# Sums over w_ada for the second layer and both gates: products by ScalarE, additions by GpSimd

## What is computed

```python
mod = jax.nn.silu(c) @ w_ada + b_ada
shift, scale, gate = jnp.split(mod[:, None, :], 3, axis=-1)
h = rms_norm(x, norm_g) * (1 + scale) + shift
z = h @ w_in                       # eight parts: queries, keys, values, gates, latents
o_mla, o_moba = ...                # two attentions of 8 heads
y = jnp.concatenate([silu(g_mla) * o_mla, silu(g_moba) * o_moba], axis=-1) @ w_out
return x + gate * y
```

## Time and profile before

| | |
|---|---|
| median of 3 runs | 1597.88 us (1596.69 to 1599.29) |
| profiled execution | 1596.89 us |
| its span, first to last instruction | 1594.7 us |
| TensorE busy | 1552.5 us (97%) |
| VectorE busy | 1069.9 us (67%) |
| ScalarE busy | 869.8 us (55%) |
| GpSimd busy | 117.0 us (7%) |
| chain that ended last | PE 88%, DVE 5%, ACT 3%, issue 2%, DMA 1% |
| loads of w_ada | 48 of 512 KB, median 5.3 us from issue to landing |

### The profile page before, as it was taken

How to read it: one execution, slowest core, us unless ns; L and a number is a source line. 1 busy time by engine, 2 the same in 40 slices (tenths; PEclk the granted TensorE clock), 3 DMA queues, 4 the chain that set the end, 5 groups by cost and what they waited for, 6 DMA issues and landing times.

```text
span 1594.7 us, 21371 instructions
## 1 busy us (share of the span) xinstructions
PE 1552.5 (97%) x7540; PEld 1290.8 (81%) x7540; DVE 1069.9 (67%) x1789; ACT 869.8 (55%) x1534; POOL 117.0 (7%) x142
## 2 busy tenths in 40 slices
PE   4989999999999999999999999999999999999998
PEld 4777887788888888888888888888888888888886
DVE  7987877666555766787756557565666578766553
ACT  3676667455445656565644446444566666554442
POOL 0310021011000000021000001000000002100000
PEclk9999999999999999999999999999999999999999
DMA  9964673379854634546565557975463444665651
GB/s 340 322 233 158 196 239 128 104 180 221 222 185 158 198 96 133 174 141 213 197 200 170 198 184 197 199 205 192 158 199 118 139 160 147 211 207 172 205 184 71
DMA packets 149026, 293.03 MB, mean 184 GB/s; under 512 B 10096, under 2 KB 23184, under 8 KB 148920
## 3 DMA queue, kind: packets, MB, share of 16 engines
q1 hardware_dynamic: 143424, 276.60, 51.5%
q0 software_dynamic: 4352, 12.15, 6.2%
q10 hardware_dynamic: 1144, 2.92, 0.5%
HBM read 290.57 MB, written 1.06 MB: 183 GB/s over the span
## 4 chain that ended last, share of the span: by engine, by line
PE 88%; DVE 5%; ACT 3%; issue 2%; DMA 1%; POOL 0%; DVEq 0%; SPq 0%; ACTq 0%
PE pb L475 83%; PE pb L479 5%; DMA raw<-in_w_ada 1%; DVE wl L1529 1%; ACT wh L906 1%; ACT pb L906 1%; DVE mkv L1526 1%; POOL st L2461 0%; DMA raw<-in_w_in 0%; DVE qt L1526 0%; ACT xt_h L906 0%; DVE mk L1529 0%; ACT mkv L906 0%; DVE B L1529 0%; DVE pb L1532 0%
## 5 line engine op out<-in xcount | busy, mean ns | idle before, releaser
L906 ACT ACTIVATE wh<-raw 128x1024 fp32r<-128x1024 f32 (+1 forms) x484 | 506.5, 1053 | 424.6 <-PE pb L475 394.2
L1529 DVE TENSOR_TENSOR wl<-raw,wh 128x1024 fp32r<-128x1024 f32 (+1 forms) x484 | 581.4, 1218 | 197.6 <-ACT wh L906 193.6
L475 PE MATMUL pb<-wh,xt_h 128*128 128x512 f32 (+2 forms) x1472 | 578.1, 393 | 4.0 <-ACT xt_h L906 2.5
L475 PE MATMUL pb<-wh,xt_l 128*128 128x512 f32 (+2 forms) x1472 | 572.4, 389 | 1.4 <-DVE xt_l L1529 1.0
L475 PE MATMUL pb<-wl,xt_h 128*128 128x512 f32 (+2 forms) x1472 | 569.6, 387 | 0.0
L475 PEld LDWEIGHTS pb<-wh,xt_l 128*128 128x128 f32 x1472 | 277.1, 188 | 64.1 <-DVE xt_l L1526 5.9
L475 PEld LDWEIGHTS pb<-wh,xt_h 128*128 128x128 f32 x1472 | 277.2, 188 | 59.5 <-issue 4.0
L475 PEld LDWEIGHTS pb<-wl,xt_h 128*128 128x128 f32 x1472 | 277.4, 188 | 52.5
L475 PE MATMUL pb<-wh,big_h 128*128 128x512 f32 x352 | 137.7, 391 | 0.0
L475 PE MATMUL pb<-wh,big_l 128*128 128x512 f32 x352 | 137.0, 389 | 0.0
L475 PE MATMUL pb<-wl,big_h 128*128 128x512 f32 x352 | 137.0, 389 | 0.0
(11 more groups left out here) (242 smaller groups left out, 1546.5 us busy)
## 6 DMA issues: line engine op xcount, KB each, us to landing
raw<-in_ffn_w_gu SPq DMA_DIRECT2D x160, 512.0 KB, 4.9
raw<-in_w_in SPq DMA_DIRECT2D x148, 512.0 KB, 4.3
raw<-in_ffn_w_down SPq DMA_DIRECT2D x88, 512.0 KB, 3.9
raw<-in_w_ada SPq DMA_DIRECT2D x48, 512.0 KB, 5.3
raw<-in_w_out SPq DMA_DIRECT2D x32, 512.0 KB, 4.1
raw<-in_w_branch SPq DMA_DIRECT2D x24, 512.0 KB, 4.2
raw<-in_ffn_w_gu SPq DMA_DIRECT2D x32, 256.0 KB, 4.9
raw<-in_w_in SPq DMA_DIRECT2D x8, 416.0 KB, 4.8
```

The source lines that it names most:

```text
L475: return e.matmul(o, a, b, start=start, stop=stop)
L906: return e.activation(o, a, func, **kw)
L1529: return e.tensor_tensor(o, a, b, op)
```

## The change

The tiles (0, 0) and (0, 2) stay as they are. For the four others, 32 rows, the work moves from VectorE to two engines. ScalarE multiplies a row by its weights (`weigh` in act): for kx = 0 into the accumulator, for the others in place, raw into raw; the signal is ("prod", l, j, kx). It stands in ScalarE's queue where the row stands in the plan, right behind the copy of the entry before it. GpSimd adds raw to the accumulator for kx = 1 to 7 (`sums`), signal ("accp", l, j, kx); for kx = 0 it only waits for the product. A buffer is free for the next load after "prod" for kx = 0 and after "accp" for the others. Where the additions stand in GpSimd's order is written out by hand: SUMS gives for each layer how many rows are done after the rs of rn, before those of qb, before those of kb, before those of mq, and after the load of the gate's bias: 4, 2, 2, 9, 7 in the first layer and 3, 1, 2, 2, 0 in the second. What TensorE waits for before it adds up over the partitions is changed accordingly.

```diff
--- before.py
+++ after.py
@@ -399,12 +399,16 @@
 
     def weighed(l, j, kx):
 
-        return ("acc", l, j + 1 if j < 4 and l == 0 and kx == 7 else j, kx)
+        if (l, j) in ((0, 0), (0, 2)):
+            return ("acc", l, j + 1 if kx == 7 else j, kx)
+        return ("accp", l, j, kx) if kx else ("prod", l, j, 0)
 
     def first_bank_of(c):
 
         return {0: 2, 2: 3, 4: 7}.get(c)
 
+
+    SUMS = ((4, 2, 2, 9, 7), (3, 1, 2, 2, 0))
 
     def moba_unit(l):
         def f(hh, t):
@@ -666,7 +670,7 @@
             if j >= 4:
                 return
             b = rot("mod", l, j)
-            w.wait_ge(*at("acc", l, j // 2 * 2 if l else j, 7))
+            w.wait_ge(*(at("accp", l, j // 2 * 2, 7) if l else at("acc", l, j, 7)))
             w.wait_ge(*at("ones"))
             a = acc_of[l, j // 2 * 2][:, j % 2 * 512:j % 2 * 512 + 512]
             for f in range(4):
@@ -763,7 +767,7 @@
             later.drain(0 if l else 8)
             for j2 in range(2):
                 o = open_bank(first_bank + j2, ("gate", l, j2))
-                w.wait_ge(*at("acc", l, 4, 7))
+                w.wait_ge(*at("accp", l, 4, 7))
                 mm(o, ones[:, :], acc_of[l, 4][:, j2 * 512:j2 * 512 + 512], True, True).then_inc(*up("turn", l, 4 + j2))
             side.drain()
             later.over(7)
@@ -913,11 +917,23 @@
             for c in chunks:
                 src, kk, n, _, i, ada_ = plan[c]
                 if ada_:
+                    if ada_[0:2] not in ((0, 0), (0, 2)):
+                        weigh(c)
                     continue
                 w.wait_ge(*at(f"raw{c % NRAW}", c))
                 if i >= NW:
                     w.wait_ge(*at(*plan[split_at[i - NW]][3]))
                 ac_(wh[i % NW][:, 0:kk * n], raw[c % NRAW][:, 0:kk * n]).then_inc(*up("hi", c))
+
+        def weigh(c):
+
+            l, j, kx = plan[c][5]
+            v = raw[c % NRAW][:, :]
+            w.wait_ge(*at(f"raw{c % NRAW}", c))
+            w.wait_ge(*at("csil"))
+            if kx == 0 and (l, j) in acc_free:
+                w.wait_ge(*at(*acc_free[l, j]))
+            ac_(v if kx else acc_of[l, j], v, scale=stat(8, "c_silu")[:, kx:kx + 1]).then_inc(*up("prod", l, j, kx))
 
         def turn_of_temp(reader):
 
@@ -1540,7 +1556,8 @@
             for c in chunks:
                 src, kk, n, _, i, ada_ = plan[c]
                 if ada_:
-                    weigh(c)
+                    if ada_[0:2] in ((0, 0), (0, 2)):
+                        weigh(c)
                     continue
                 w.wait_ge(*at("hi", c))
                 if i >= NW:
@@ -1553,17 +1570,14 @@
 
 
             l, j, kx = plan[c][5]
-            first = l == 0 and j < 4
             v, a = raw[c % NRAW][:, :], acc_of[l, j]
             weight = stat(8, "c_silu")[:, kx:kx + 1]
             w.wait_ge(*at(f"raw{c % NRAW}", c))
             if kx == 0:
-                if (l, j) in acc_free:
-                    w.wait_ge(*at(*acc_free[l, j]))
                 ts(a, v, weight, None, ALU.mult, None).then_inc(*up("acc", l, j, 0))
                 return
             w.wait_ge(*at("acc", l, j, kx - 1))
-            if kx < 7 or not first:
+            if kx < 7:
                 stt(a, v, weight, a, ALU.mult, ALU.add).then_inc(*up("acc", l, j, kx))
                 return
             for z in range(2):
@@ -2477,6 +2491,19 @@
                 e.dma_start(bc[:, a0:a0 + n], bass.AP(tensor=d[name].tensor, offset=0, ap=[[0, 128], [1, n]])).then_inc(
                     *landed(to))
 
+        def sums(n):
+
+            for _ in range(n):
+                c, (l, j, kx) = rows_left.popleft()
+                w.wait_ge(*at("prod", l, j, kx))
+                if kx > 1:
+                    w.wait_ge(*at("accp", l, j, kx - 1))
+                if kx:
+                    a = acc_of[l, j]
+                    e.tensor_tensor(a, a, raw[c % NRAW][:, :], ALU.add).then_inc(*up("accp", l, j, kx))
+
+        rows_left = deque((c, p[5]) for c, p in enumerate(plan) if p[5] and p[5][0:2] not in ((0, 0), (0, 2)))
+
         e.memset(ones[:, :], 1.0).then_inc(*up("ones"))
         e.memset(cols[:, 126:128], -0.5).then_inc(*up("half"))
         e.memset(gp[:, :], 1.0).then_inc(*up("gpone"))
@@ -2487,6 +2514,7 @@
         for l in range(NL):
             for t in range(2):
                 rstd(1, "rn", l, t)
+            sums(SUMS[l][0])
             for t in range(2):
                 rstd(1, "zq", l, t)
                 rstd(1, "zk", l, t)
@@ -2497,10 +2525,12 @@
                 e.dma_start(gv, bass.AP(tensor=scratch.tensor, offset=0, ap=[[1, 128], [512, 8], [1, 256]])).then_inc(
                     *landed("gv"))
             for nm in ("qb", "kb"):
+                sums(SUMS[l][1 if nm == "qb" else 2])
                 for t in range(2):
                     rstd(8, nm, l, t)
                 if l == 0 and nm == "qb":
                     vectors(bc_in[:2], "bcm")
+            sums(SUMS[l][3])
             for nm in ("mq", "mk"):
                 for t in range(2):
                     rstd(8, nm, l, t)
@@ -2508,6 +2538,7 @@
             w.wait_ge(*at("tr", ("mlak", l), 6))
             e.dma_start(gate, bass.AP(tensor=b_.tensor, offset=b_.offset + 2 * DM, ap=[[0, 128], [1, DM]])).then_inc(
                 *landed("bgate", l))
+            sums(SUMS[l][4])
 
         def bias_table(s, l):
```

## The result

The changed kernel takes 1618.84 us (median of 4 runs, 1616.96 to 1619.68), the kernel before 1598.59 beside it on the same chip: ratio 1.0125, 95% interval 1.0107 to 1.0142, so some 20 us slower. The forecast was slower by 10, and the range ended at 1618: the direction was right, the size half of what came. The profiled execution has a span of 1615.1 us.

The account below looks back on a forecast made before the run. The prediction took TensorE's chain as the bound, with its waits in the first layer from 80 us on deciding. Terms 3.5 + 4.8 − 1.3 + 2.4 + 1.0 = 10.4 on 1596.9 gave 1607 us, range 1597 to 1618.

Parts of the forecast that it names:

- The lock between GpSimd and VectorE: Two-input VectorE instructions and GpSimd instructions reading SBUF exclude each other for their full length; counted as nothing in the sum.
- Rival (a): The lock decides: seven additions after 83 us hold five splits, +6.5 on top, 1614 us; chance 0.17.
- Before 80 us a short delay is swallowed.: Before 80 us the weight splits are some microseconds ahead of TensorE, so a short delay costs nothing.
- The 10 us that VectorE saves in 40 to 80: Eight rows' VectorE time saved in 40 to 80 us; claimed no help while the keys wait for a load.
- First term: Buffers freed only after GpSimd's additions delay loads of 54.44 and 59.30, so keys reach TensorE late: +3.5, bounds 0 to 6.
- Second term: ScalarE, without idle time between 83 and 98 us, takes five w_ada products there: +4.8, bounds 3 to 5.3.
- the fifth: Second layer: one row falls into the same full ScalarE stretch as in the first: +1.0, bounds −1 and 2.
- The five products: Sign to look for: five ScalarE products among the evictions of 83 to 98 us.
- Third term: The multiply-add at 121.34 directly ahead of VectorE's mk goes, shortening TensorE's wait at 125.38: −1.3, bounds −2.5 and 0.
- Fourth term: Seven additions behind the gate's load free a buffer late; ScalarE waits for w_ada near 134 us: +2.4, bounds 0 and 4.
- Faster rival (b): VectorE was the limiter and ScalarE's products find gaps; waits and half the clock cost go: 1593 us, chance 0.15.
- Rival (c): Near nothing: buffers in time, ScalarE at its lower bound, waits at 82.29 and 125.38 go: +1.5, 1598 us, chance 0.13.

Follow-up runs that it names:

- e3: Changed kernel with each GpSimd addition cut to 8 of 1024 columns, sums incomplete: 1609.40 us, ratio 1.0070.
- e4: Changed kernel with two memsets of the accumulator, about 1.97 us together and reading nothing, in place of each GpSimd addition: 1609.95 us, ratio 1.0074.
- e5: As e4, but a buffer is free for its next load at once after ScalarE's product: 1610.64 us, ratio 1.0076.
- e13: Changed kernel with two memsets in place of each of the seven additions of tile (1, 0) alone: 1612.30 us, ratio 1.0084.
- e7: Changed kernel with 28 rows narrowed: ScalarE's products to 8 columns, additions replaced by two 8-column memsets: 1603.50 us, ratio 1.0032.
- e10: As e7, but a buffer is free at once after ScalarE's product: 1598.64 us, ratio 1.0002.
- e8: Only tile (1, 4) moved to ScalarE and GpSimd, the other three left with VectorE as in the kernel before: 1599.63 us, ratio 1.0012.
- e6: Changed kernel with VectorE adding in place of GpSimd and ScalarE's 28 in-place products cut to 8 columns: 1599.99 us, ratio 1.0013.
- e11: Only tile (1, 2) moved, others left with VectorE, one addition put ahead of GpSimd's wait for mlak: 1599.62 us, ratio 1.0004.
- e14: Changed kernel with two memsets in place of the very first GpSimd addition alone: 1615.65 us, ratio 1.0108.

## Why the prediction came out at half the size

**The lock between GpSimd and VectorE (counted at nothing, measured 8.2 to 8.8).** This step failed, and it is nearly the whole miss of 9.6 us: the sum was 10.4, and without reading additions the kernels e3, e4 and e5 show 11.2 to 12.1. The rows for it were there, and the prediction names the rule. The reasoning "I count nothing, since VectorE also loses 1.28 per row" set off time on VectorE against time on VectorE. What TensorE pays for is the moment: an addition can hold the instruction that VectorE has next, up to its full length. Rival (a) had the mechanism and nearly the size (+6.5) but the wrong place, so its size is luck: it looked for it after 83 us, and the runs put most of it before 80 (e13), and the traces of after and e4 all of it. After 83 VectorE was there first. The changed kernel's additions of the tiles (0, 4) and (1, 4), duration in ns min/median/max:

```profile
L2503 POOL TENSOR_TENSOR acc<-acc,raw x14: 2345/2408/6608, 87.9 to 253.5; 128x1024 f32<-128x1024 f32 x14
```

The longest is the one of 87.9. VectorE runs one instruction with two inputs after the other from 87.01 to 92.30, each of its usual length:

```profile
87.01 2.28 DVE L1545 TENSOR_TENSOR mbias<-sg,cst 128x2048 f32<-128x2048 f32 x1
...
91.02 1.28 DVE L1545 TENSOR_TENSOR wl<-raw,wh 128x512 fp32r<-128x512 f32 x2
```

The addition ends at 94.5, some 2.2 us behind the last of them. So here the addition was held, and VectorE wasn't.

**"Before 80 us a short delay is swallowed."** Wrong for delays of this length. In the changed kernel, VectorE beside GpSimd again:

```profile
72.59 1.22 DVE L1545 TENSOR_TENSOR wl<-raw,wh 128x1024 fp32r<-128x1024 f32 x1 [1.65 <-ACT wh L910]
73.73 2.79 DVE L1539 TENSOR_SCALAR ang<-ang 128x32 f32<-128x32 f32 x1
76.56 0.18 DVE L1849 CAST ang<-ang 128x32 int32<-128x32 f32 x1
76.78 2.29 DVE L1851 CAST ang<-ang 128x32 f32<-128x32 int32 x1
...
80.11 1.23 DVE L1545 TENSOR_TENSOR wl<-raw,wh 128x1024 fp32r<-128x1024 f32 x1
```

```profile
74.06 4.97 POOL L2503 TENSOR_TENSOR qt<-qt,raw 128x1024 f32<-128x1024 f32 x2
```

The two held instructions take 0.17 and 0.18 us in the trace of before. Together they lose 4.7 us, more than the splits were ahead: the split of 80.11 had stood at 69.90 before, and TensorE waits 1.60 us for it at 81.39. A part of its lateness is from earlier delays and from ScalarE's late copy (the 1.65 us ahead of 72.59), but e13, with memsets there and buffers as late, has no such wait. The 10 us that VectorE saves in 40 to 80 don't help, since they are saved at other moments.

**First term, late buffers (+3.5).** The mechanism was right: the loads of the earlier trace rows at 54.44 and 59.30 went out at 66.09 and 68.64 (11.7 and 9.3 later; 11 and 9 were predicted), the copy of 69.02 at 76.46 (76). Its price alone is 4.8 us (e7 − e10), inside its bounds. But it doesn't add to the second term: with whole products it is worth nothing that can be measured (e4, e5). Both delay the same evictions near 82 us, and it seems that the later one counts.

**Second term, ScalarE (+4.8), with the fifth, the second layer (+1.0).** Together 5.8, measured 11.8 (e5 − e10): this is the second step that failed, a term of half its size. By the table of delays e5 less e10 is 8.6 at number 800 and 11.6 at 1250, so some 9 us are the first layer's and 3 the second's; tile (1, 4) alone, additions included, costs 1.9 (e8). The five products were found as predicted; in e5 they start at 89.09, 95.47, 99.79 (two) and 104.80. Left out were the products just ahead of that stretch, at 79.02 and 82.89, and with them the evictions for the transposes that come 2.7 us later. Left out too was the clock: after these waits 80 to 100 runs at 0.83 instead of 0.91 and 100 to 120 at 0.83 instead of 1.00. Between numbers 250 and 400 e5 takes 10.3 us more than e10. TensorE waits 5.7 us more there, and it is at the lower clock for 10.3 us more, which is worth up to half of that, 5.1. So about half of the loss is waits, near the term's 4.8, and the other half the clock behind them; that split is worked out from the traces, not measured by itself. The prediction used a price for the clock in its faster rival only, and never on the side of loss.

**Luck in the rest of the sum.** That the sum without the lock comes within 2 us of e3, e4 and e5 is luck, since its errors have opposite signs: the first and the fourth term (5.9) were added in full, where one is free beside whole products and the other worth half, and the second and fifth together were 6 too small.

**Third term (−1.3).** The number is right: TensorE's wait for mk is gone, and the delay shrinks by 1.7 between numbers 450 and 500. The reason is not shown. In e10, where the multiply-add is gone too, 0.45 us of the wait are left, and in e6, where VectorE adds up the same row in 1.22 us just ahead of mk, the wait is gone as well. Tile (1, 2) by itself (e11) brings nothing, +0.6 with an interval across zero.

**Fourth term (+2.4).** Half of it, in the place named. ScalarE waits for the row, in the changed kernel's timeline, and TensorE stands behind it:

```profile
150.97 1.15 ACT L910 ACTIVATE raw<-raw,st 128x1024 f32<-128x1024 f32 x1 [1.11 <-DMA raw<-in_w_ada]
```

```profile
152.44 0.71 PE L479 MATMUL pb<-kt,qt 96*128 96x128 f32 x4 [1.52 <-ACT pt L910]
```

The delay grows by 1.2 between numbers 500 and 800. With the buffers free at once (e5) TensorE waits no longer there than before, 1.9 us in all, and 2.9 in e4, so the mechanism is right. That only half came may be because earlier delays leave the load more time, an effect that the term's lower bound named.

**Faster rival (b).** e10 speaks against it: with VectorE relieved and next to nothing for the others to do, the time is that of before. VectorE's 19.48 of 20 was fullness without a gain behind it, and yet no room for more. Rival (c), near nothing, needed buffers in time and products among waits. e10 has the first, and short products in place of the second; with whole products no kernel with all 32 rows came out there.

## What to carry over

Work moved to an idle engine isn't priced by that engine's time but by what its instructions hold while they run: write down, for each stretch, what the neighbour has next and how far ahead of the critical engine it is, and compare that lead with the full length of the holder. Most of the 28 additions cost TensorE little or nothing; the few that met VectorE without a lead cost it waits of 1.83 and 1.60 us (after) and 4.08 us (e14). A wait of the critical engine can cost its own length and then as much again at the lower clock behind it (here 3.5 us of waits and 6.8 us at 1.2 GHz before number 250), so both belong into every term of loss. Terms that delay the same wait are not simply added.

## What the runs showed of the hardware

While a GpSimd addition that reads two tiles runs, even very small VectorE instructions wait for its end: a TENSOR_SCALAR of 128x32, 0.17 us in the trace of before, took 2.79 and 2.88; a CAST of 128x32, 0.18 before, took 2.29 and 2.24. These have one input. A GpSimd MEMSET, which reads nothing, held the same instructions for its own length: casts of 0.96 and 0.97 us beside memsets of 0.97 and 0.96 (e4). The Trainium skill (SBUF — State Buffer, section on who interferes with whom) names both kinds: VectorE instructions with two SBUF inputs, and `tensor_scalar` and casts where they run in a mode that uses both ports. The traces agree on both, with the numbers just given for the second kind, though no row tells in which mode those ran, and 2.78 instead of 0.76 us for the subtractions. The same section says that a GpSimd instruction that only writes SBUF doesn't hold a VectorE instruction with two inputs. The trace of e4 agrees: 0.76 us for the two subtractions and 2.36 for two splits beside memsets.

A GpSimd addition of 128x1024 took 2.35 us at its shortest and 2.41 in the median. The mean of 2.90 for 14 of them comes in good part from the one of 6.61 that VectorE held: the hold works in both directions. VectorE's splits had a mean of 1219 ns beside memsets (e4), and 1249 ns in the changed kernel: over 484 of them 14.2 us more busy time, and the small instructions held are on top of that.
